# The RWKV scan of a hybrid backbone: one joined 128-token step against two 64-token halves in sequence

## The reference, cut to what matters

```
def step(s, inp):
    w_t, k_t, v_t, kk_t, b_t = inp[:5]
    sa = jnp.einsum("bhvk,bhk->bhv", s, -kk_t)
    s = s * w_t[:, :, None, :] + sa[..., None] * b_t[:, :, None, :] + v_t[..., None] * k_t[:, :, None, :]
    y = jnp.einsum("bhvk,bhk->bhv", s, inp[5]) if readout else None
    return s, y
```

## Time and profile before

| | us |
|---|---|
| three timed runs | 2820.0, 2826.18, 2826.22 (median 2826.18) |
| the profiled execution's own time | 2821.89 |
| span of its trace | 2820.1 |
| PE busy in the span | 2575.1 (91%) |
| DVE, ACT, POOL busy | 777.5, 649.8, 599.2 |
| mean granted TensorE clock | 0.957 |
| scan of layer 0, first score to last read-out | 294.5 to 517.6 |
| scan of layer 1 | 1334.1 to 1541.1 |

### The profile page before, as it was taken

The page is one execution under the profiler, slowest core; times in us unless marked ns, Lnnn a source line. Parts: engine busy times, 40 slices in busy tenths (PEclk is TensorE's granted clock), DMA queues, the critical chain, the costliest instruction groups (busy, mean ns, idle before and its releaser), DMA issues.

```text
span 2820.1 us, 60215 instructions
## 1 busy us (share of the span) xinstructions
PE 2575.1 (91%) x27302; PEld 1622.7 (58%) x27302; DVE 777.5 (28%) x1390; ACT 649.8 (23%) x1003; POOL 599.2 (21%) x398
## 2 busy tenths in 40 slices
PE   5997899679999999696998699999999999999997
PEld 3773688457777778483787544444444444444444
DVE  2126555533222223527544420001000000000002
ACT  2232554332222222343553310000000000000001
POOL 4333533233333334154532300000000000000000
PEclk9998899899999999897999899999999999999998
DMA  7541000323444443121001489889898989898990
GB/s 241 180 142 37 36 3 3 105 75 119 150 148 151 145 154 98 51 83 41 3 3 48 160 333 371 317 335 358 328 370 313 378 309 382 305 370 318 376 360 29
DMA packets 197702, 544.80 MB, mean 193 GB/s; under 512 B 6704, under 2 KB 80704, under 8 KB 191808
## 3 DMA queue, kind: packets, MB, share of 16 engines
q1 hardware_dynamic: 193728, 528.50, 51.0%
q10 hardware_dynamic: 3712, 12.24, 1.2%
HBM read 535.47 MB, written 5.24 MB: 192 GB/s over the span
## 4 chain that ended last, share of the span: by engine, by line
PE 48%; issue 2%; DVE 1%; ACT 1%; DMA 0%; POOL 0%; POOLq 0%; ACTq 0%; DVEq 0%; SPq 0%
PE bank L719 24%; PE bank L722 12%; PE bank L692 1%; PE bank L1729 1%; PE bank L1725 1%; PE bank L1701 1%; PE bank L710 1%; PE bank L707 1%; PE bank L750 1%; PE bank L1740 1%; PE bank L1785 1%; PE bank L1799 1%; DMA arena<-in_w_out_dram 0%; PE bank L1710 0%; PE bank L1622 0%
## 5 line engine op out<-in xcount | busy, mean ns | idle before, releaser
L719 PE MATMUL bank<-arena 128*32 128x512 f32 (+1 forms) x6624 | 829.5, 560 | 36.2 <-issue 34.8
L722 PE MATMUL bank<-arena 128*32 128x256 f32 (+1 forms) x6624 | 516.2, 363 | 0.0
L306 POOL TENSOR_TENSOR w_lo<-arena,w_hi 128x2048 fp32r<-128x2048 f32 x78 | 354.7, 4548 | 603.6 <-ACT w_hi L300 603.5
L722 PEld LDWEIGHTS bank<-arena 128*32 128x32 f32 x6624 | 224.3, 110 | 417.2 <-issue 387.1
L316 PE MATMUL bank<-h_hi,w_hi 128*128 128x512 f32 (+1 forms) x1008 | 388.5, 385 | 49.0 <-DVE h_lo L1223 41.3
L318 PE MATMUL bank<-h_hi,w_lo 128*128 128x512 f32 (+1 forms) x1008 | 376.6, 374 | 0.0
L317 PE MATMUL bank<-h_lo,w_hi 128*128 128x512 f32 (+1 forms) x1008 | 374.4, 371 | 0.0
L719 PEld LDWEIGHTS bank<-arena 128*32 128x32 f32 x6624 | 224.6, 110 | 180.3 <-issue 65.2
L316 PEld LDWEIGHTS bank<-h_hi,w_hi 128*128 128x128 f32 x1008 | 193.3, 192 | 115.7 <-issue 61.2
L634 DVE TENSOR_TENSOR arena<-arena,bank 128x768 f32<-128x768 f32 (+2 forms) x45 | 31.3, 713 | 723.0 <-ACT arena L509 723.0
L318 PEld LDWEIGHTS bank<-h_hi,w_lo 128*128 128x128 f32 x1008 | 192.6, 191 | 35.9
(11 more groups left out here) (270 smaller groups left out, 2656.3 us busy)
## 6 DMA issues: line engine op xcount, KB each, us to landing
arena<-in_moe_w_dram SPq DMA_DIRECT2D x189, 2048.0 KB, 9.7
arena<-in_w_mod_dram SPq DMA_DIRECT2D x48, 1024.0 KB, 5.0
arena<-in_ffn_w_dram SPq DMA_DIRECT2D x42, 1024.0 KB, 7.1
arena<-in_w_in_dram SPq DMA_DIRECT2D x26, 1024.0 KB, 6.2
arena<-in_w_out_dram SPq DMA_DIRECT2D x8, 1024.0 KB, 13.7
x_store<-arena ACTq DMA_DIRECT2D x2, 2048.0 KB, 7.5
arena<-x_store ACTq DMA_DIRECT2D x2, 2048.0 KB, 8.5
arena<-in_ctx_dram ACTq DMA_DIRECT2D x1, 1024.0 KB, 11.2
```

What stands on the lines that cost most here:

```text
L306: pool.tensor_tensor(lo, slot_view(splits[i][0]), hi, ALU.subtract).then_inc(sem("w_lo"), 1)
L719: mm(bank[b][64 * h + 32 * c:64 * h + 32 * c + 32, 0:n // 2], xa[:, 32 * c:32 * c + 32], w[:, n // 2 * h:n // 2 * (h + 1)], start=first, s ...
L722: ins = mm(bank[b + 1][blk(q), 0:n // 4], xb, w[:, n // 4 * q:n // 4 * (q + 1)], start=first, stop=last)
```

## The change

**Halves in sequence.** The two inverses are no longer joined. The halves are called `z` = 0 and 1 in order of time, and `i` is the half of the tile (i = z forward, 1 - z backward). For each, PE does `enter_state` (state into the sum, and into the read-out), `z_sum`, `solve`, `read`; ACT copies in (`z_in`) and out (`z_out`); DVE adds to the state and to Y. All of this stands twice in a step, and the second half waits for the state of the first. Every product is on a 64 x 64 part of the array.

**Scores.** Only the diagonal 64 x 64 blocks are computed, with the four parts in turn, b vectors and keys in one call per group. `corner` is one copy and not three; `masked_s1` and `masked_s2` become `masks`, on half the elements.

**Joining goes.** `join_x`, `join_u`, `joined` and four half copies go. In their place `turn_last` transposes the last T (four transposes in all) and `turned_last` copies it, once per group. POOL no longer adds the identity nor clears `TF`; DVE adds the identity in `first_t`.

**Memory.** `MC` holds 64 columns and no zero blocks. The buffers are small enough for `X` to stay: the write to `x_store`, the load back and the waits for them go.

**Order.** The solve and read of `st - 1` are spread over levels 1 to 3, the scores of `st + 1` move from levels 3 and 4 to before and after `level_x(4)`, and `turn_keys` goes to levels 4 and 5. On DVE `bonus` moves from level 2 to the step's end. On ACT `stage` of `st + 2` stands behind `z_in` and `z_out` of the second half.

```diff
-        x_store = nc.dram_tensor("x_store", [P, KD, T], fp32).ap()
...
-        MC = area(o_stage + 3584, NP, P)
+        MC = area(o_stage + 3584, NP, HS)
...
-                act.dma_start(x_store, X).then_inc(sem("x_out"), 16)
...
-                    for i in range(2):
-                        act.activation(lc[half(i)], sc[half(i), :, :, half(i)], ACT.Copy)
-                    act.activation(sx[src], sc[src, :, :, dst], ACT.Copy).then_inc(sem("act_lc"), 1)
...
+                    act.activation(lc, sc[:, :, :, 0:HS], ACT.Copy).then_inc(sem("act_lc"), 1)
...
+                    act.activation(wk[q]["ZI"], ps[:, 4 * q + 2:4 * q + 4, 2 * P:3 * P], ACT.Copy).then_inc(sem("act_zi"), 1)
...
+                    act.activation(wk[q]["ZS"][half(i)].rearrange("s h p n -> s h (p n)"),
+                                   ps[half(i), 4 * q + 2:4 * q + 4, 3 * P:4 * P], ACT.Copy).then_inc(sem("act_z"), 1)
...
+                    act.activation(wk[q]["TF"], ps[:, 4 * q:4 * q + 2, P:2 * P], ACT.Copy).then_inc(sem("act_t5"), 1)
...
-                act.dma_start(X, x_store).then_inc(sem("x_in"), 16)
...
+                    for j in range(2):
+                        for p in range(2):
+                            for i, h in ((0, 0), (1, 1), (0, 1), (1, 0)):
+                                c = 256 * p + P * j
+                                ins = mm(bank[b + h][half(i), c:c + HS * nar].rearrange("s (a n) -> s a n", a=nar),
+                                         (BS, KS)[j][half(h), 2 * q + p, half(i)],
+                                         AR[cn % 3][half(h), 2 * q + p, 0:nar, half(i)], start=True, stop=True)
...
+                    for p, h in pairs:
+                        ins = mm(zi[h][:, p], AR[cn % 3][half(h), 2 * q + p, 0, half(i)], MC[half(h), 2 * q + p],
+                                 start=(p == 0), stop=False, skip_group_check=True)
+                    for p, h in pairs if reads_out(l, st) else ():
+                        ins = mm(y_[h][:, p], MC[half(h), 2 * q + p], AR[cn % 3][half(h), 2 * q + p, 1, half(i)],
+                                 start=False, stop=False, skip_group_check=True)
...
+                    for p, h in pairs:
+                        ins = mm(zi[h][:, p], w["S2"][cn % 2][half(i), 2 * h + p, 0],
+                                 VTK[half(i), TILE(st), 2 * q + p, half(h)],
+                                 start=(p == 0 and not has_state(st, z)), stop=True, skip_group_check=True)
...
+                    for p, h in pairs:
+                        ins = mm(pk(4 * q + 2 + h, 8, HS)[half(i), 6 + p], w["TF"][half(h), p, half(i)],
+                                 w["ZI"][half(h), h, half(p)], start=(p == 0 and h != i), stop=True,
+                                 skip_group_check=True)
...
+                    for p, h in pairs:
+                        mm(m_[half(h), 4 + p], w["BK"][cn % 2][half(i), 2 + p, half(h)], tok[:, p, half(h)],
+                           start=(p == 0), stop=False, skip_group_check=True)
+                    for p, h in pairs:
+                        ins = mm(m_[half(h), 4 + p], w["BK"][cn % 2][half(i), p, half(h)], w["ZS"][half(i), h, p],
+                                 start=False, stop=True, skip_group_check=True)
...
+                    if z:
+                        link(nc.vector.tensor_tensor(mt[:, pq], m_, m_new, ALU.add))
+                        ins = nc.vector.tensor_tensor(m_, mt[:, pq], fac[:, st // 4, pq, st % 4].unsqueeze(2)
+                                                      .to_broadcast([P, 2, HS]), ALU.mult)
+                    elif st % 4:
+                        ins = nc.vector.tensor_tensor(m_, m_, m_new, ALU.add)
```

More of the change, by code:

```diff
@@ L354, in hybrid_kernel @@
             for st_ in range(8):
[L355 to L358, removed]
+                for i_ in range(4):
+                    un += st_ % 4 != 3 or i_ < 2
+                    updates[l_, st_, i_] = un
+        UTOT = [updates[l_, 7, 3] for l_ in range(L)]
         def CTOK(l, ct):
@@ L871, in _ @@
                 link(ins)
+            link(nc.gpsimd.tensor_copy(above[:], tri[:, 0]))
+            for i in range(2):
+                link(nc.gpsimd.tensor_copy(tri_c[half(i)], tri[half(i), :, half(i)]))
             for d in range(2):
@@ new lines, in read_out @@
+                    tok = slice(TILE(st) * P + HS * i, TILE(st) * P + HS * i + HS)
+                    dve.wait_ge(sem("pe_y"), 4 * ybefore[l, st] + 2 * z + q + 1)
+                    for h in range(2):
+                        y_ = Y[half(h), 2 * q:2 * q + 2, tok]
+                        y_new = pk(4 * q + 2 + h, 8, HS)[half(h), i:4:2]
+                        if st < 4:
+                            ins = nc.vector.tensor_copy(y_, y_new)
+                        else:
+                            ins = nc.vector.tensor_tensor(y_, y_, y_new, ALU.add)
@@ L1834, in _ @@
                 wait(pe, "mod_cols", 3 * l + 3)
                 pe.wait_ge(sem("vtok"), NT * (l + 1))
[L1836 to L1838 removed]
+                for q in range(2):
+                    score(0, q)
                 for q in range(2):
@@ L1851, in _ @@
+                        z_sum(st - 1, 1, 0)
                     level_u(st, 2)
                     if st:
-                        read(st - 1, 1)
+                        enter_state(st - 1, 1, 1)
+                        solve(st - 1, 1, 0)
+                        z_sum(st - 1, 1, 1)
                     level_x(st, 3)
+                    if st:
+                        solve(st - 1, 1, 1)
+                        read(st - 1, 1, 0)
+                    level_u(st, 3)
+                    if st:
+                        read(st - 1, 1, 1)
@@ L1866, in _ @@
                     level_x(st, 5)
-                    z_sum(st, 0)
-                    level_u(st, 5)
-                    z_sum(st, 1)
-                    join_x(st)
-                    if st < 7:
-                        turn_keys(st + 1, 0)
-                    join_u(st)
+                    enter_state(st, 0, 0)
                     if st < 7:
                         turn_keys(st + 1, 1)
-                for q in range(2):
-                    solve(7, q)
-                for q in range(2):
-                    read(7, q)
+                    level_u(st, 5)
@@ new lines, in _ @@
+                    z_sum(st, 0, 0)
+                    enter_state(st, 0, 1)
+                    turn_last(st)
+                    z_sum(st, 0, 1)
+                for z in range(2):
+                    for q in range(2 if z else 0):
+                        enter_state(7, 1, q)
+                    for q in range(2 if z else 0):
+                        z_sum(7, 1, q)
+                    for q in range(2):
+                        solve(7, z, q)
+                    for q in range(2):
+                        read(7, z, q)
```

392 lines of the change are left out of this document (166 added, 226 removed).

## The result

The kernel after takes **2729.9 us** (median of four runs, 2728.0 to 2734.1), the kernel before beside it 2826.2 (2820.0 to 2827.8). The ratio is 0.9665, with a 95% interval of 0.9647 to 0.9684: 3.4% faster. The forecast was 2760, with a range of 2742 to 2792. The profiled execution took 2728.8 itself, against 2821.9 before: 93.1 us less.

The account below looks back on a forecast made before the run. PE was taken to bound the scan, so removed products are time gained. Terms summed to 64.4 us off the profiled 2821.9, giving 2757.5; half of a 4.3 us offset on top made 2760, range 2742 to 2792.

Parts of the forecast that it names:

- better still: Rival for the new scan's products: the array parts overlap better than L1760 and no wait shows; 2731 us, chance 0.05.
- layer 0, six middle steps: Layer 0's scan: full steps of 24.1 us in place of 27.15, so 143 against 162.9, -20 us.
- layer 0, first step: Layer 0's first scan step, from 22.2 us: cheaper scores and sums, no join, added transposes; -5.4 us.
- layer 0, start: Start of layer 0's scan: 6.45 us in place of 8.86, second score call no longer waiting for masks; -2.4 us.
- layer 0, last step and `w_out`: End of layer 0: last step unchanged, first `w_out` unit landing earlier without the residual's load; -5.45 us.
- layer 1, six middle steps: Layer 1's scan, cheaper without read-out: 132.6 us against 150.9, -18.3 us.
- layer 1, first step, start: Beginning of layer 1's scan: first step -4.3 us and start -2.2 us.
- issue of the store: ACT no longer issues the residual's store ahead of `stage`, which starts the scan; -0.9 us for both layers.
- Prices: PE products: 67 ns on two parts in turn, 134 on one; score call 0.95 us; full layer 0 step 23.0 us.
- The row-group rule: Rival in `z_sum` and `read`: products in one row group fail to overlap, 134 ns each; 2818 us, chance 0.04.
- Waits: PE's waits in a full step: level 3's copy 0.6, `enter_state` 0.2, group 1's `first_t` 0.3; together 1.1 us.
- The load: Without the residual's load back, the first `w_out` unit lands in 5.4 us, not 10.87; -10.9 us over both layers.

Follow-up runs that it names:

- run with 32 transposes: Kernel after plus 32 PE transposes of the identity, read by nothing, between layer 1's scan and the group norm: 2759.4 us.
- `pairs`: Kernel after with the four products of each half-step group ordered head 0, 0, 1, 1 in place of 0, 1, 0, 1: 2736.5 us.
- `both`: Kernel after with DVE's bonus operations behind level 2's sums and ACT's `stage` cut in two, its first part between the second half's `z_in` copies: 2711.3 us.
- run `bonus`: Kernel after with DVE's two bonus operations moved from the step's end to behind level 2's sums: 2723.2 us.

## Why the prediction was wrong

**The term that is missing.** The working stops where the scan and its residual end, and takes all behind them as unchanged. That was the failing step: no term for what the change does to the code behind it. Its price is 25.4 us of the 30. Of the rest, 2.3 are behind the last item's start, 1.0 in front of the loop, and 2.5 were put on top of the profiled time; against this, the median lies 1.1 above the profiled run. That something could change there could have been asked from the diff alone: PE's program grows by 3008 records, and a loop of 3122 stands behind it. That there was something to lose stood in the trace of before, under PE's waits:

```profile
PE bank L719 <- issue: 34.8, 14, 3.9
```

Whether the change would take any of it away could not be read from there. With the items measured here, 125.3 to 132.0 us against 129.4, the range should have been open by some 29 us below and 18 above (an estimate from seven items). How little the scan had to do with it shows the run with 32 transposes: the kernel after in a bad place took 2759.4 us, of which 0.7 are the longer way from the last step to the loop (118.3 us in place of 117.6). That this is the forecast's number is chance. So is it that the rival "better still", 2731, has the measured time: it wanted some 30 us more from the scan, which gave 65.4.

**The scan, by its terms.** In front of the expert loop 64.4 were forecast and 65.4 came.

| term | forecast | measured |
|---|---|---|
| layer 0, six middle steps | -20 | -19.1 |
| layer 0, first step | -5.4 | -4.0 |
| layer 0, start | -2.4 | -2.2 |
| layer 0, last step and `w_out` | -5.45 | -6.9 |
| layer 1, six middle steps | -18.3 | -21.1 |
| layer 1, first step, start | -6.5 | -5.5 |
| layer 1, last step and `w_out` | -5.45 | -7.0 |
| issue of the store | -0.9 | +0.3 |

Against the fair partner, the kernel before with 32 transposes (2792.0), the kernel after is 62 us faster. The transposes cost that partner nothing up to the loop: 124.6 us from its last step to the loop, with and without.

- *Prices.* Two parts in turn: 67 ns taken, 58 measured (0.23 us for four, L1808 and L1811 at the end of layer 0). One part alone is 117 ns and not 134 (`pairs`). Sixteen score products take 0.88 us to the next group's start, not 0.95:

```profile
336.15 1.06 PE L1690 MATMUL bank<-arena 64*64 64x128 f32 x32
337.03 0.64 PE L1728 MATMUL bank<-arena 64*64 64x64 f32 x32
...
490.42 0.40 PE L1811 MATMUL bank<-arena 64*64 64x64 f32 x8
490.65 0.40 PE L1808 MATMUL bank<-arena 64*64 64x64 f32 x8
490.88 0.40 PE L1811 MATMUL bank<-arena 64*64 64x64 f32 x8
```

A full step of layer 0 keeps PE busy for 22.1 us in place of 23.0, and lasts 23.33 in place of 24.1:

```profile
366.36:389.69 23.33, 22.07 (x674) 18.50 (x673) 14.68 (x37) 13.04 (x28) 9.59 (x13) 1.00 0.02 5
```

- *The row-group rule.* In these read-outs the row group never changes within a group, and the products still run at 58 ns, half the 117 of one part. Between the rule of the Trainium skill, "TensorE: Matmul & The Clock Gate", "Part 3: Packing small matmuls", and L1827, that decides in favour of the row.
- *Waits.* By the same row they are 1.3 us a full step, forecast 1.1:

```profile
368.68 0.46 PE L1728 MATMUL bank<-arena 64*64 64x64 f32 x16 [0.25 <-ACT arena L1065]
374.17 0.45 PE L1770 MATMUL bank<-arena 64*64 64x64 f32 x8 [0.45 <-DVE arena L1405]
378.56 0.95 PE L1728 MATMUL bank<-arena 64*64 64x64 f32 x32 [0.53 <-ACT arena L1065]
```

The one at level 3, behind `stage`, is 0.53 us for 0.6 forecast, though its repair gave 0.95 (`both`); `enter_state` waits 0.45 for 0.2; the third is level 1's copy, and not `first_t`, for 0.25 and 0.3. `bonus` was put at 0.5 us in all. In the profiled run it cost 2.8 and 3.7 us in steps 5 and 6 of layer 0, against the run `bonus`: 1.2 of each goes with the wait at the full clock, and what PE's clock does behind the wait was not counted. So in layer 0 products that were priced too dear, 0.8 us a step, hid that `bonus` was priced too low, and the -19.1 looks better than its parts.
- *Layer 1* gained 2.8 us more than forecast, with nothing of that kind against the lower price of the products: its steps 5 and 6, 21.5 and 21.2 us, have no half clock behind `bonus`, which costs 1.2 and 1.1 us there (20.3 and 20.1 in the run `bonus`).
- *The load* came at its price (5.1 us for 10.9). The issue of the store was worth nothing.

## What to carry to other kernels

When a change alters how many instructions an engine has ahead of a long loop, measure the loop by itself in both kernels, and compare each with some dummy instructions ahead of it, before anything is put down to the change. An idle time of PE put down to "issue" at a loop's start is a sign that there is something to gain. Where DVE or ACT have work that is not urgent, it belongs where they wait, not at the end of a step where it reads well: `bonus` and `stage` in such places gave 18.6 us, over a quarter of the 65.4 that the rewrite of the scan gave. A wait of PE is to be priced with what its clock does behind it.

## What the runs showed of the hardware

- PE's loop of 3122 records an item stands still for 1.9 to 4.2 us at each jump back, wherever it lies (the jump's own record takes 3.3 to 5.6 us), and for up to 4.9 us more a little later, where its program crosses into the next 16 KB before they have landed. The padding ahead of the loop decides: items of 125.3 to 132.0 us, with a period of 256 records.
- fp32 products of 64x64 with 64 columns take 117 ns each on one part of the array (L1772, L1753), 58 on two parts, be it in one row group, and in either order of the products (L1808 of the kernel after and of `pairs`), and 39 on four (L1740).
- PE's granted clock fell to half behind a wait of 1.17 us within a busy stretch in the kernel after, and behind the same wait it did not with 32 transposes (clock 1.00). Layer 0's first step took 17.6 to 21.4 us in the ten kernels with the same code there. With a fall, in `bonus`; the kernel after had 18.21 us at 1.00:

```profile
302.10:323.47 21.37, 20.11 (x432) 14.91 (x433) 11.97 (x23) 10.45 (x20) 12.58 (x16) 0.68 0.01 4
```
